# The opening of a three-block transformer kernel reordered, with the third block's position bias computed in it

## Chip, cores and metric

The kernel runs on one core of a Trainium2 chip. The metric is the device time of one execution in microseconds. Before the change it is 779.05 us, the median of 3 runs (778.85 to 779.05).

## The reference

256 tokens of width 1024 (`x`) and 256 context tokens (`ctx`) go through two attention blocks with adaptive norms, and the result through a third block:

```
shift, scale, gate = adaln(c, ada_w[i], ada_b[i])         # silu(c) @ w + b, three parts
h  = rms_norm(x, pre_g[i]) * (1.0 + scale) + shift        # hc likewise from ctx and c_ctx
q, k, v, z = split(h @ a_w_in[0])                         # block 1: differential attention, rope
x = x + gate * rms_norm(y, post_g[i])
...
bias = rel_bias[t5_bucket(idx - qpos)]                    # block 3: bias of the sparse attention
```

The change touches block 1's opening (modulation, first norm, first projection `h @ a_w_in`), the order of its loads, and the matmul that turns `rel_bias` (32 x 8) into one row of 512 position biases for each head. What is computed is the same.

## The kernel before, in words

All matmuls of projections are three products of rounded parts (fp32r): an operand is rounded (`act_hi`, `w_hi`) and its rest kept (`act_lo`, `w_lo`); hi by hi, hi by lo and lo by hi are summed in PSUM. ScalarE writes the `w_hi`, VectorE the `w_lo`.

Work goes by chunks of 512 weight columns. A chunk's weights come in two halves of 512 rows (1 MiB each). Stage `in0` is block 1's input projection: eight chunks, each for four token tiles (0 and 1 are x, 2 and 3 the context) and eight row blocks k. A unit (c, t) is chunk c for tile t, 24 matmuls. Chunks 1 to 4 (`BY_FEATURES`) hold queries and keys: their units come out by features, and VectorE rotates them (`rotate0`, `rest_x`).

Loads: SP issues them in the order of `loads_plan` into `RAW` = 6 buffers. Load n goes to buffer n % 6 and waits in `stream` (L631) until load n - 6 has been used, by the table `emptied` (L587 to L598): the first half of an `in0` chunk is used when its last tile has done k = 3, the second when the chunk's last unit is done. `ada1` is the modulation of block 2: four chunks of two loads, each multiplied by TensorE in `ada_half` (L879) after the unit that `BESIDE_IN0` names. It needs no rounding. `ada0g` is block 1's gate, summed on VectorE by `gate_block` (L2266).

The halves are rounded in the order in which they are used, at fixed places in the queues of ScalarE and VectorE: in `unit_in0` a chunk's first unit is followed by the split of the first half of the next chunk, and `run_chunk` puts the split of its second half ahead of the chunk's last unit. Both engines work in the order written. So whoever waits for a half there holds all units behind it.

```
emptied, firsts = {}, 0
for n, (stage, c, h) in enumerate(loads):
...
    if n >= RAW:
        sp.wait_ge(*emptied[n - RAW])
...
    if t == 0:
        split_through(half_no[("in0", c, 0)] + 2)
```

In the opening chunk 0 is woven by hand (L1024 to L1054) with block 1's modulation `ada0`: four chunks n, each in two halves (`ada_half`), giving shift and scale for the row blocks 2n and 2n + 1. For each n the norm of x and of the context is transposed (`norm0_part`, L1011), the modulation rows are copied by ScalarE and turned into columns (`mod_columns`, L914), VectorE adds the biases (`first_sums`, L2154), ScalarE applies them (`first_hi`, L1449), VectorE takes the rest (`first_lo`, L2174), and only then can TensorE multiply these two blocks. `round_block` (L1466) and `split_block` (L2190) round chunk 0's weights by row block. `stay_awake` (L997) are filler matmuls with zeroes, whose result nobody reads.

The bias of block 3 is a matmul at L1195, ahead of the chunk `in2` 0. Its one-hot matrix is loaded before `in2`'s first load, `rel_bias` in POOL's list (L1990), ScalarE copies the result (`toep`, L1807) and SP writes it to DRAM, from where it is read back in overlapping rows.

Of the kernel before, what the change touches and what calls it, by code (L numbers as in the profile page):

```python
# [14 lines left out]
KT = D // P  # L15
# [44 lines left out]
BESIDE_IN0 = {(c, 3): ("ada1", c) for c in range(4)}  # L60


COLUMNS_IN0 = (4, 1)
# [96 lines left out]
def banks_plan():  # L160
# [33 lines left out]
    for i, (s, n) in enumerate([(0, 0), (0, 1), (1, 0), (1, 1), (0, 2), (1, 2), (0, 3), (1, 3)]):  # L194
        put(("norm0", s, n), 2 + i % 3)
    for t in range(NT):
        put(("in0", 0, t), [0, 1, 7, 5][t])
    for c in range(6):
        for t in range(NT):
            if c in BY_FEATURES:  # L200
                put(("in0", c, t), 2 + t)
            elif c:
                gemm_unit("in0", c, t)
            if (c, t) == (0, 3):
                put(("ada1", 3, 0), 6)
            elif (c, t) == COLUMNS_IN0:
                put(("mod1",), 7)
# [41 lines left out]
    put(("bias",), 6)  # L249
# [50 lines left out]
def block_kernel(nc, a, out):  # L300
# [7 lines left out]
    with ctx:  # L308
# [81 lines left out]
        onehot = v_flat[0:32, 3072:3584]  # L390
        toep = v_flat[0:HEADS, 3584:4096]
# [59 lines left out]
        N_CIN, N_VEC, N_LATE = 3, 4, 10  # L451
# [173 lines left out]
        def _(sp):  # L625
# [26 lines left out]
            load(ident[:], a["k_ident"], s_cin)  # L652
            modulation(0)
            stream(0)
            for t in range(XT):
                load(xs[:, XT + t, :], a["ctx"][0, t * P:(t + 1) * P, :], s_ctxin)
            modulation(1)
            modulation(2)
            stream(1)
            modulation(3)  # L660
            for n in range(2, RAW):
                stream(n)
            for n in range(RAW, len(loads)):
                if loads[n] == ("ada1", 1, 0):

# [24 lines left out]
                if loads[n] == ("in2", 0, 0):  # L690

                    b, at = place[("pv1", XT * HEADS - 1)]
                    sp.wait_ge(full[b], at + 1)
                    load(onehot, a["k_onehot"], s_onehot)
                if loads[n] == ("in2", 3, 0):

                    b, at = place[("bias",)]
                    sp.wait_ge(free[b], at + 1)
                    sp.dma_start(toep_dram, toep).then_inc(s_toepw, 16)
# [121 lines left out]
        def _(pe):  # L821
# [211 lines left out]
            for t in range(XT):  # L1033
                gemm_unit("in0", 0, t, ks=range(0, 2))
            ada_half("ada0", 1, 0)
            stay_awake(5, 4)
            for n in range(2):
                norm0_part(n, 1)
            for n in range(1, 4):
                before = range(2 * n - 2, 2 * n)  # L1040
                ada_half("ada0", n, 1)
                if n > 1:
                    for s in range(2):
                        norm0_part(n, s)
                gemm_unit("in0", 0, 2, ks=before)
                mod_columns(0, n)
                if n < 3:
                    ada_half("ada0", n + 1, 0)
                gemm_unit("in0", 0, 3, ks=before)
                if n < 3:  # L1050
                    for t in range(XT):
                        gemm_unit("in0", 0, t, ks=range(2 * n, 2 * n + 2))
            for t in range(XT):
                gemm_unit("in0", 0, t, ks=range(6, KT))  # L1054
# [137 lines left out]
            pe.wait_ge(s_late, 16 * N_LATE)  # L1192
            pe.wait_ge(s_onehot, 16)
            o = begin(("bias",))
            pe.matmul(o[0:HEADS, :], relb[:], onehot, start=True, stop=True).then_inc(bank_full(("bias",)), 1)  # L1195
# [216 lines left out]
        def _(act):  # L1412
# [53 lines left out]
            def round_block(h, kk):  # L1466


                g, at = h, load_no[halves[h]]
                act.wait_ge(landed[at % RAW], landed_at[at])  # L1470
# [56 lines left out]
            round_block(0, 2)  # L1527
            round_block(0, 3)
            act.wait_ge(s_ctxin, 16 * XT)
            norm0_square(2)  # L1530
            norm0_square(3)
            first_hi(0, 1)
            move(mod_rows(0, 1), ("ada0", 1, 0), n=P)
            first_hi(1, 0)
            first_hi(1, 1)
# [26 lines left out]
            def unit0(c, t):  # L1562
# [7 lines left out]
                if (c, t) == (HALF_KT, 0):  # L1570
                    move(mod_rows(1, HALF_KT - 1), ("ada1", HALF_KT - 1, 0))
# [235 lines left out]
            move(toep, ("bias",))  # L1807
# [153 lines left out]
        def _(pool):  # L1961
# [19 lines left out]
            for dst, src in ((sel[:], a["k_sel"]), (lamb[:], a["a_lambda"][0].partition_broadcast(P)),  # L1981
# [4 lines left out]
                             (w_ukv[:, 0, :], a["w_uk_2"][0]), (w_ukv[:, 1, :], a["w_uv_2"][0]),  # L1986
                             (relb[:], a["rel_bias_2"])):
# [6 lines left out]
        def _(dve):  # L1994
# [179 lines left out]
            def first_lo(n, s):  # L2174
                name = ("norm0", s, n)
                tokens = tile_cols(XT * s, XT)
                dve.wait_ge(*seq.last)
                for i, k in enumerate((2 * n, 2 * n + 1)):
                    if i:
                        dve.wait_ge(s_hi0, feature0_no(s, k) + 1)  # L2180
                        seq.freed(dve.tensor_scalar(sc[:, 4 + k % 4, tokens], psum[:, place[name][0], tile_cols(XT * i, XT)],
                                                    mod[:, 0, 0, k, s:s + 1], mod[:, 0, 1, k, s:s + 1], ALU.mult, ALU.add)
                                  .then_inc(bank_free(name), 1), name)
                        dve.wait_ge(*seq.last)
                    else:
                        dve.wait_ge(s_f0, 2 * n + s + 1)
                    seq.note(dve.tensor_tensor(act_lo[:, k, tokens], sc[:, 4 + k % 4, tokens], act_hi[:, k, tokens].bitcast(F32),  # L2187
                                               ALU.subtract).then_inc(s_lo0, 1), s_lo0)
# [14 lines left out]

            first_sums(0)
            split_block(0, 0)
            split_block(0, 1)
            first_lo(0, 0)
            split_block(0, 2)
            split_block(0, 3)
            norm_in("norm0", range(XT, NT))  # L2210
            first_lo(0, 1)
            first_sums(1)
            first_lo(1, 0)
            first_lo(1, 1)
# [3 lines left out]
            first_lo(2, 0)  # L2218
            first_lo(2, 1)
# [3 lines left out]
            first_lo(3, 0)  # L2223
            first_lo(3, 1)
# [41 lines left out]
            def gate_block(c, s, k):  # L2266
# [3 lines left out]
                if kk == 0 and not s:  # L2270
# [3 lines left out]
                    elif not h:  # L2274
                        dve.wait_ge(s_gatein, 32)
                w = raw_view(load_no[("ada0g", c, h)])[:, kk, :] if c else gate_place[h][:, kk, :]
# [753 lines left out]
```

## Time and profile before

| | us |
|---|---|
| median of 3 runs | 779.05 |
| the profiled execution's own time | 778.93 |
| its span, first to last instruction | 776.8 |
| TensorE busy | 765.9 (99%) |
| VectorE busy | 550.8 (71%) |
| ScalarE busy | 392.8 (51%) |

The busy times are of one profiled execution. Matmuls are pipelined, so their busy time counts overlaps and is no measure of the array at its peak. SPq is the time in which SP issues a transfer, not the transfer. "DMA share" is the mean busy share of the core's 16 DMA engines.

### The profile page before, as it was taken

What the parts mean: (1) busy time and instruction counts of PE and PEld (TensorE: products, weight loads), DVE (VectorE), ACT (ScalarE), POOL (GpSimd) and SP (SyncE); (2) the same over time, 40 slices, a digit from 0 to 9 for tenths busy, and PEclk for the clock granted to TensorE, in tenths of its full rate; (3) what the DMA queues carried; (4) which work ended last, traced back from release to release, by engine and by line L of the source; (5) the groups of instructions that cost most, each with busy time, mean ns of one, the idle gap of its engine ahead of it and who ended that gap; (6) DMA issues with size and microseconds to landing.
All of it is one profiled execution on the core that took longest, in us unless ns stands there. A gap on an engine that the chain in (4) does not pass through costs nothing.

```text
span 776.8 us, 11220 instructions
## 1 busy us (share of the span) xinstructions
PE 765.9 (99%) x4137; PEld 614.1 (79%) x4137; DVE 550.8 (71%) x985; ACT 392.8 (51%) x749; POOL 42.0 (5%) x55
## 2 busy tenths in 40 slices
PE   8999999999999999999999999999999999999998
PEld 6668777887777788867788888787788888888886
DVE  3455998987677867599757766998977554554553
ACT  4462223338788765556656656634444444434341
POOL 0120000000001010111100002200100000000000
PEclk9999999999999999999999999999999999999999
DMA  9995555333000085149221054963325845665611
GB/s 326 360 381 186 212 217 189 113 122 118 2 1 1 1 327 209 60 162 349 70 94 58 9 183 166 376 203 107 109 66 178 271 163 165 206 209 181 205 63 55
DMA packets 72409, 125.78 MB, mean 162 GB/s; under 512 B 2842, under 2 KB 36844, under 8 KB 71204
## 3 DMA queue, kind: packets, MB, share of 16 engines
q1 hardware_dynamic: 71504, 123.00, 45.8%
q10 hardware_dynamic: 388, 1.08, 0.4%
q0 software_dynamic: 464, 0.98, 0.4%
q8 instruction: 34, 0.56, 0.3%
q14 instruction: 19, 0.16, 0.1%
HBM read 123.99 MB, written 1.06 MB: 161 GB/s over the span
## 4 chain that ended last, share of the span: by engine, by line
PE 83%; DVE 8%; ACT 3%; DMA 3%; issue 2%; SPq 0%; POOL 0%; DVEq 0%; ACTq 0%
PE psum L871 18%; PE psum L873 17%; PE psum L872 16%; PE psum L1067 3%; PE psum L1092 3%; DMA raw<-in_a_w_in 3%; PE psum L993 3%; PE psum L1387 3%; PE psum L1388 3%; PE psum L1386 3%; PE psum L860 2%; PE psum L1165 2%; PE psum L861 2%; PE psum L862 2%; DVE w_lo L2004 2%
## 5 line engine op out<-in xcount | busy, mean ns | idle before, releaser
L872 PE MATMUL psum<-w_lo,act_hi 128*128 128x512 f32 (+1 forms) x624 | 242.0, 388 | 0.0
L871 PE MATMUL psum<-w_hi,act_hi 128*128 128x512 f32 (+1 forms) x584 | 237.5, 407 | 2.6 <-DVE act_lo L2187 2.4
L873 PE MATMUL psum<-w_hi,act_lo 128*128 128x512 f32 (+1 forms) x584 | 227.0, 389 | 0.0
L2004 DVE TENSOR_TENSOR w_lo<-raw,w_hi 128x2048 fp32r<-128x2048 f32 (+1 forms) x68 | 153.2, 2261 | 62.1 <-ACT w_hi L1425 62.1
L1425 ACT ACTIVATE w_hi<-raw 128x2048 fp32r<-128x2048 f32 (+1 forms) x72 | 136.3, 1896 | 65.5 <-PE psum L873 30.9
L871 PEld LDWEIGHTS psum<-w_hi,act_hi 128*128 128x128 f32 x584 | 109.7, 188 | 37.2 <-issue 13.3
L872 PEld LDWEIGHTS psum<-w_lo,act_hi 128*128 128x128 f32 x624 | 117.5, 188 | 20.5 <-issue 0.5
L873 PEld LDWEIGHTS psum<-w_hi,act_lo 128*128 128x128 f32 x584 | 109.6, 188 | 23.4
L1973 POOL TENSOR_TENSOR rstd<-ms,half_neg 128x1 f32<-128x1 f32 (+3 forms) x38 | 35.5, 936 | 520.6 <-DVE ms L2045 520.5
L860 PE MATMUL psum<-act_hi,w_hi 128*128 128x512 f32 x128 | 50.6, 395 | 0.5 <-DVE w_lo L2004 0.5
L861 PE MATMUL psum<-act_lo,w_hi 128*128 128x512 f32 x128 | 50.0, 390 | 0.0
L862 PE MATMUL psum<-act_hi,w_lo 128*128 128x512 f32 x128 | 49.8, 389 | 0.0
L1583 ACT ACTIVATE sc<-psum,nmax 128x512 f32<-128x512 f32 (+1 forms) x64 | 36.8, 587 | 20.3 <-DVE nmax L2320 20.3
L1498 ACT ACTIVATE sc<-psum 128x512 f32<-128x512 f32 (+1 forms) x59 | 30.8, 523 | 16.3 <-PE psum L993 9.2
L2320 DVE TENSOR_REDUCE nmax<-psum 128x2 f32<-128x1024 f32 (+1 forms) x32 | 30.5, 955 | 10.3 <-PE psum L1067 10.2
L1387 PE MATMUL psum<-w_lo,act_hi 128*128 128x512 f32 x88 | 34.2, 389 | 0.0
L1929 ACT ACTIVATE sc<-psum 128x256 f32<-128x256 f32 x22 | 8.4, 384 | 50.5 <-PE psum L873 50.5
L860 PEld LDWEIGHTS psum<-act_hi,w_hi 128*128 128x128 f32 x128 | 24.0, 188 | 9.2 <-issue 3.4
L1386 PE MATMUL psum<-w_hi,act_hi 128*128 128x512 f32 x80 | 31.2, 390 | 0.0
L1388 PE MATMUL psum<-w_hi,act_lo 128*128 128x512 f32 x80 | 31.1, 389 | 0.0
L993 PE MATMUL psum<-ident,sc 128*128 128x128 f32 x184 | 29.5, 274 | 0.4 <-ACT sc L1884 0.4
L1092 PEld LDWEIGHTS psum<-vbuf,sc 128*128 128x128 f32 x192 | 26.1, 191 | 4.0 <-ACT sc L1498 0.9
(295 smaller groups left out, 1124.7 us busy)
## 6 DMA issues: line engine op xcount, KB each, us to landing
raw<-in_a_w_in SPq DMA_DIRECT2D x16, 1024.0 KB, 9.3
raw<-in_ada_w SPq DMA_DIRECT2D x14, 1024.0 KB, 5.2
raw<-in_w_out SPq DMA_DIRECT2D x12, 1024.0 KB, 5.5
raw<-in_w_gate SPq DMA_DIRECT2D x22, 512.0 KB, 4.1
raw<-in_w_up SPq DMA_DIRECT2D x22, 512.0 KB, 5.2
raw<-in_w_down SPq DMA_DIRECT2D x11, 1024.0 KB, 4.9
raw<-in_b_w_in SPq DMA_DIRECT2D x10, 1024.0 KB, 7.6
raw<-in_w_in SPq DMA_DIRECT2D x10, 1024.0 KB, 6.1
```

The lines of the kernel that those rows point to most:

```text
L860: pe.matmul(o, hi[:, tile_cols(t)], act_hi[:, k, :], start=(k == 0), stop=False)
L861: pe.matmul(o, hi[:, tile_cols(t)], act_lo[:, k, :], start=False, stop=False)
L862: mm = pe.matmul(o, lo[:, tile_cols(t)], act_hi[:, k, :], start=False, stop=(k == KT - 1))
L871: pe.matmul(oh, x_hi, hi, start=(k == 0), stop=False)
L872: pe.matmul(o[:, 0:n], x_hi, lo, start=False, stop=False)
L873: mm = pe.matmul(oh, x_lo, hi, start=False, stop=(k == KT - 1))
L993: mm = pe.transpose(o[:, tile_cols(i)], src[:, tile_cols(i)], ident[:])
L1386: pe.matmul(oh, x_hi, hi, start=(j == 0 and i == 0), stop=False)
L1387: pe.matmul(o, x_hi, lo, start=False, stop=False)
L1388: mm = pe.matmul(oh, x_lo, hi, start=False, stop=(last and i == 1))
L1425: ins = act.activation(hi, weights, ACTF.Copy)
L2004: ins = dve.tensor_tensor(rest, weights, hi.bitcast(F32), ALU.subtract)
```

## The change

- `BESIDE_IN0` puts the four `ada1` chunks behind in0's chunks 1 to 4 instead of 0 to 3. `loads_plan` follows it, so the order of loads moves too. The column turn of `ada1` goes from behind unit (4, 1) to behind (5, 1).
- The first weight half comes in two transfers of 0.5 MiB, rows k = 0 and 1 before the context, k = 2 and 3 behind the second `ada0` chunk; the first has a semaphore of its own.
- SP's opening: chunk 1 of in0 now stands before `ada1`, the gate's first chunk before `ada1` 0.
- TensorE's opening: units by row block, then tile (`first_units`); x's units of a row block before, the context's behind the modulation; four fillers less. ScalarE and VectorE are put in the same order.
- The bias: one-hot and `rel_bias` are loaded by SP behind the context, into `gate0`; the matmul stands in the opening in PSUM bank 5, with copy and write behind it. `gate_block` waits for the write.

```
-BESIDE_IN0 = {(c, 3): ("ada1", c) for c in range(4)}
+BESIDE_IN0 = {(c + 1, 3): ("ada1", c) for c in range(4)}
-COLUMNS_IN0 = (4, 1)
+COLUMNS_IN0 = (5, 1)
...
-        onehot = v_flat[0:32, 3072:3584]
-        toep = v_flat[0:HEADS, 3584:4096]
+        onehot = gate0[0:32, 1, 0:COLS]
+        toep = gate0[0:HEADS, 1, COLS:]
...
             modulation(0)
-            stream(0)
+            sp.dma_start(raw_view(0)[:, 0:2, :], first[:, 0:2, :]).then_inc(s_firstin, 16)
             for t in range(XT):
                 load(xs[:, XT + t, :], a["ctx"][0, t * P:(t + 1) * P, :], s_ctxin)
+            load(relb[:], a["rel_bias_2"], s_onehot)
+            load(onehot, a["k_onehot"], s_onehot)
             modulation(1)
+            sp.dma_start(raw_view(0)[:, 2:4, :], first[:, 2:4, :]).then_inc(landed[0], 16)
             modulation(2)
             stream(1)
             modulation(3)
-            for n in range(2, RAW):
-                stream(n)
-            for n in range(RAW, len(loads)):
-                if loads[n] == ("ada1", 1, 0):
+            b, at = place[("bias",)]
+            sp.wait_ge(free[b], at + 1)
+            sp.dma_start(toep_dram, toep).then_inc(s_toepw, 16)
+            for n in range(2, len(loads)):
+                if loads[n] == ("ada1", 0, 0):
...
+            X, CONTEXT = range(XT), range(XT, NT)
+            first_units(X, (0, 1))
             ada_half("ada0", 1, 0)
-            stay_awake(5, 4)
...
+            pe.wait_ge(s_onehot, 32)
+            o = begin(("bias",))
+            pe.matmul(o[0:HEADS, :], relb[:], onehot, start=True, stop=True).then_inc(bank_full(("bias",)), 1)
+            norm0_part(0, 1)
+            ada_half("ada0", 1, 1)
+            norm0_part(1, 1)
+            mod_columns(0, 1)
+            first_units(CONTEXT, (0, 1))
+            first_units(X, (2,))
+            ada_half("ada0", 2, 0)
+            first_units(X, (3,))
+            ada_half("ada0", 2, 1)
...
+            mod_columns(0, 3)
+            first_units(CONTEXT, (4, 5))
+            first_units(X, (6, 7))
```

Three places show how instructions moved. The first is SP's queue from chunk 4 of in0 to the first half of chunk 6 (rows on `raw` with 128x4x512 from `in_a_w_in` are in0's halves; `in_ada_w` with 128x2048 is `ada1`, with 128x4x512 `ada0g`). Before:

```order
L638 DMA raw<-in_ada_w 128x2048 [waits w_first_half_used]
L638 DMA raw<-in_ada_w 128x2048 [waits bank5_full]
L638 DMA raw<-in_a_w_in 128x4x512 [waits ada_first_half_used] x2
L638 DMA raw<-in_ada_w 128x4x512 [waits w_first_half_used]
L638 DMA raw<-in_ada_w 128x4x512 [waits bank5_full]
L638 DMA raw<-in_a_w_in 128x4x512 [waits ada_first_half_used]
L638 DMA raw<-in_a_w_in 128x4x512 [waits bank6_full]
L638 DMA raw<-in_a_w_in 128x4x512 [waits w_first_half_used]
```

And in the change:

```order
L639 DMA raw<-in_a_w_in 128x4x512 [waits ada_first_half_used] x2
L639 DMA raw<-in_ada_w 128x2048 [waits w_first_half_used]
L639 DMA raw<-in_ada_w 128x2048 [waits bank5_full]
L639 DMA raw<-in_ada_w 128x4x512 [waits ada_first_half_used] x2
L639 DMA raw<-in_a_w_in 128x4x512 [waits w_first_half_used]
L639 DMA raw<-in_a_w_in 128x4x512 [waits bank5_full]
L639 DMA raw<-in_a_w_in 128x4x512 [waits ada_first_half_used]
```

Before, chunk 5's two halves (sixth and seventh row) wait for an `ada1` pair, and chunk 6's first half (last row) for the first-half use of chunk 4. Now chunk 5's first half is the one that waits for the first-half use (fifth row), and chunk 5's second half for the end of chunk 4's last unit in bank 5.

The second place is TensorE behind the first four units of chunk 0 (`kT` holds the modulation's second chunk). Before:

```order
L908 MATMUL psum<-kT,cstat 32x128 [waits bank6_free,ada0_landed2]
L908 MATMUL psum<-kT,cstat 32x128 x15
L1001 MATMUL psum<-w_hi 128x512 x4
L1019 MATMUL psum<-ident,zbuf 128x128 [waits xn_ready]
L1019 MATMUL psum<-ident,zbuf 128x128 x3
L1019 MATMUL psum<-ident,zbuf 128x128 [waits bank2_free,xn_ready]
L1019 MATMUL psum<-ident,zbuf 128x128 x3
L908 MATMUL psum<-kT,cstat 32x128 [waits ada0_landed3]
```

And in the change:

```order
L904 MATMUL psum<-kT,cstat 32x128 [waits bank6_free,ada0_landed2]
L904 MATMUL psum<-kT,cstat 32x128 x15
L1039 MATMUL psum<-gate,relb 8x512 [waits onehot_in]
L1015 MATMUL psum<-ident,zbuf 128x128 [waits xn_ready]
L1015 MATMUL psum<-ident,zbuf 128x128 x3
L904 MATMUL psum<-kT,cstat 32x128 [waits ada0_landed3]
L904 MATMUL psum<-kT,cstat 32x128 x15
L1015 MATMUL psum<-ident,zbuf 128x128 [waits bank2_free,xn_ready]
L1015 MATMUL psum<-ident,zbuf 128x128 x3
L917 MATMUL psum<-ident,gate 128x128 [waits bank6_free]
```

The bias matmul stands where the fillers stood, and the column turn (last row) directly behind the modulation's second half.

The third is ScalarE from unit (4, 0) of in0 on, in the change (`round_k` from PSUM is a unit's context part, from `sc` the x part of the unit before):

```order
L1567 ACTIVATE round_k<-psum 128x256 [waits bank2_full]
L1428 ACTIVATE w_hi<-raw 128x2048 [waits bank5_full,raw_landed2]
L1560 ACTIVATE round_k<-sc 128x256 [waits x_features_rotated]
L1567 ACTIVATE round_k<-psum 128x256 [waits bank3_full]
L1560 ACTIVATE round_k<-sc 128x256 [waits x_features_rotated]
L1567 ACTIVATE round_k<-psum 128x256 [waits bank4_full]
L1428 ACTIVATE w_hi<-raw 128x2048 [waits w_first_half_used,raw_landed3]
```

The rounding of chunk 5's first half (second row) stands behind unit (4, 0) and ahead of (4, 1), as before the change; only the copy of `ada1`'s rows, which stood between the two, is gone from here.

## Rows read from the trace of the kernel before

**Rows 1.** Engine totals of the page: busy us, share of the span, instructions.

```profile
PE 765.9 (99%) x4137; PEld 614.1 (79%) x4137; DVE 550.8 (71%) x985; ACT 392.8 (51%) x749; POOL 42.0 (5%) x55
```

**Rows 2.** Stretches: us, busy of PE, PEld, DVE, ACT, POOL, PEclk, DMA share, GB/s.

```profile
1.47:56.75 55.28, 51.56 (x447) 37.34 (x447) 25.17 (x63) 28.63 (x52) 7.42 (x12) 1.00 1.05 363
56.75:108.00 51.25, 50.82 (x240) 38.89 (x236) 41.78 (x72) 12.56 (x19) 1.59 (x3) 1.00 0.56 211
```

**Rows 3.** TensorE's waits, then its timeline (start, us), both from 0 to 57 us.

```profile
PE psum L871 <- DVE act_lo L2187: 2.4, 3, 1.4
...
PE psum L908 <- DVE mod L2164: 0.8, 2, 0.4
...
1.47 6.42 PE L1001 MATMUL psum<-w_hi 128*128 128x512 f32 x16 [1.47 <-DVE w_hi L2113]
...
11.02 2.33 PE L1001 MATMUL psum<-w_hi 128*128 128x512 f32 x9
...
18.33 0.47 PE L871 MATMUL psum<-w_hi,act_hi 128*128 128x512 f32 x1 [1.35 <-DVE act_lo L2187]
...
22.55 1.20 PE L1001 MATMUL psum<-w_hi 128*128 128x512 f32 x4
...
54.90 1.92 PE L908 MATMUL psum<-raw,cstat 128*32 128x512 f32 x16
56.75 0.50 PE L860 MATMUL psum<-act_hi,w_hi 128*128 128x512 f32 x1
```

**Rows 4.** The chain that ended last (start, us, what), from 0 to 110 us.

```profile
4.29 11.27 DMA raw<-in_a_w_in
...
56.02 10.61 DMA raw<-in_a_w_in
...
68.61 2.30 DVE w_lo L2004
```

**Rows 5.** SP's timeline at 128 and 149 us, and landing times of each first issue.

```profile
128.49 1.23 SPq L638 DMA_DIRECT2D raw<-in_a_w_in  x2
...
raw<-in_a_w_in SPq DMA_DIRECT2D x1, 1024.0 KB, 7.0
...
149.12 0.37 SPq L638 DMA_DIRECT2D raw<-in_a_w_in  x1
...
raw<-in_a_w_in SPq DMA_DIRECT2D x1, 1024.0 KB, 5.3
```

**Rows 6.** ScalarE's timeline at 135 us, VectorE's from 138 to 175 us.

```profile
135.79 1.92 ACT L1425 ACTIVATE w_hi<-raw 128x2048 fp32r<-128x2048 f32 x1
...
138.84 2.29 DVE L2004 TENSOR_TENSOR w_lo<-raw,w_hi 128x2048 fp32r<-128x2048 f32 x1
...
144.63 0.25 DVE L2144 TENSOR_TENSOR mod<-psum,cols 128x16 f32<-128x16 f32 x2
...
145.20 1.01 DVE L2282 TENSOR_SCALAR gate<-raw,cols 128x512 f32<-128x512 f32 x2
...
151.29 2.29 DVE L2004 TENSOR_TENSOR w_lo<-raw,w_hi 128x2048 fp32r<-128x2048 f32 x1
...
174.14 0.75 DVE L2335 SCALAR_TENSOR_TENSOR sc<-sc,rinv 128x512 f32<-128x512 f32 x1
```

**Rows 7.** TensorE's timeline from 148 to 175 us.

```profile
148.93 0.39 PE L860 MATMUL psum<-act_hi,w_hi 128*128 128x512 f32 x1
...
154.37 0.39 PE L871 MATMUL psum<-w_hi,act_hi 128*128 128x512 f32 x1
...
174.95 0.66 PE L993 MATMUL psum<-ident,sc 128*128 128x128 f32 x4
```

**Rows 8.** TensorE's timeline from 466 to 476 us, and one row of VectorE's.

```profile
466.99 1.02 PE L1195 MATMUL psum<-vbuf,relb 32*8 32x512 f32 x2
...
475.74 1.09 PE L966 MATMUL psum<-ident,zbuf 128*128 128x128 f32 x8
...
474.40 1.28 DVE L2470 SCALAR_TENSOR_TENSOR zbuf<-xs,rstd,gate 128x1024 f32<-128x1024 f32 x1 [0.44 <-POOL rstd L1973]
```

More of the change, by code:

```diff
@@ L195, in banks_plan @@
         put(("norm0", s, n), 2 + i % 3)
+    put(("bias",), 5)
     for t in range(NT):
@@ L248, in banks_plan @@
         gemm_unit("out1", c, t)
-    put(("bias",), 6)
     for t in range(XT):
@@ L652, in _ @@
             load(ident[:], a["k_ident"], s_cin)
+            first = half_src(*loads[0])[0]
             modulation(0)
-            stream(0)
+            sp.dma_start(raw_view(0)[:, 0:2, :], first[:, 0:2, :]).then_inc(s_firstin, 16)
             for t in range(XT):
                 load(xs[:, XT + t, :], a["ctx"][0, t * P:(t + 1) * P, :], s_ctxin)
+            load(relb[:], a["rel_bias_2"], s_onehot)
+            load(onehot, a["k_onehot"], s_onehot)
             modulation(1)
+            sp.dma_start(raw_view(0)[:, 2:4, :], first[:, 2:4, :]).then_inc(landed[0], 16)
             modulation(2)
@@ L689, in _ @@
                     load(gain3, a["norm2_w_2"][0].partition_broadcast(P), s_gain3)
[L690 to L699, printed above, removed]
                 if loads[n] == ("in2", 5, 0):
@@ L1189, in _ @@
             gemm_unit("out1", 1, 1, SECOND)
[L1192 to L1195, printed above, removed]
             gemm_unit("in2", 0, 0)
@@ L1469, in round_block @@
                 g, at = h, load_no[halves[h]]
-                act.wait_ge(landed[at % RAW], landed_at[at])
+                if h == 0 and kk < 2:
+                    act.wait_ge(s_firstin, 16)
+                else:
+                    act.wait_ge(landed[at % RAW], landed_at[at])
                 hi, weights = (part[:, kk * COLS:(kk + 1) * COLS] for part in split_parts(g)[0][0:2])
@@ L1531, in _ @@
             norm0_square(3)
+            move(toep, ("bias",))
             first_hi(0, 1)
             move(mod_rows(0, 1), ("ada0", 1, 0), n=P)
+            round_block(0, 2)
             first_hi(1, 0)
+            round_block(0, 3)
             first_hi(1, 1)
@@ L1806, in _ @@
             split()
-            move(toep, ("bias",))
             norm_square("norm2", 1, NT + 1)
@@ L2172, in first_sums, with first_lo @@
                                                   op0=ALU.add, op1=ALU.mult).then_inc(s_mod, 1), s_mod)
-            def first_lo(n, s):
-                name = ("norm0", s, n)
+            def first_lo(n, s, block):
+                name, k = ("norm0", s, n), 2 * n + block
                 tokens = tile_cols(XT * s, XT)
-                dve.wait_ge(*seq.last)
[L2178 to L2188, printed above, removed]
+                if block:
+                    dve.wait_ge(s_hi0, feature0_no(s, k) + 1)
+                    seq.freed(dve.tensor_scalar(sc[:, 4 + k % 4, tokens], psum[:, place[name][0], tile_cols(XT, XT)],
+                                                mod[:, 0, 0, k, s:s + 1], mod[:, 0, 1, k, s:s + 1], ALU.mult, ALU.add)
+                              .then_inc(bank_free(name), 1), name)
+                else:
+                    dve.wait_ge(s_f0, 2 * n + s + 1)
+                dve.wait_ge(*seq.last)
+                seq.note(dve.tensor_tensor(act_lo[:, k, tokens], sc[:, 4 + k % 4, tokens], act_hi[:, k, tokens].bitcast(F32),
+                                           ALU.subtract).then_inc(s_lo0, 1), s_lo0)
             def split_block(h, kk):
@@ L2202, in split_block, with first_los @@
                     done_halves[0] += 1
+            def first_los(n):
+                for part in range(2):
+                    for block in range(2):
+                        first_lo(n, part, block)
             first_sums(0)
             split_block(0, 0)
+            first_lo(0, 0, 0)
             split_block(0, 1)
-            first_lo(0, 0)
+            first_lo(0, 0, 1)
+            norm_in("norm0", range(XT, NT))
+            for block in range(2):
+                first_lo(0, 1, block)
+            first_sums(1)
             split_block(0, 2)
+            first_lo(1, 0, 0)
+            first_lo(1, 0, 1)
             split_block(0, 3)
[L2210 to L2214, printed above, removed]
+            for block in range(2):
+                first_lo(1, 1, block)
             first_sums(2)
```

52 lines of the change are left out of this document (21 added, 31 removed).

## The prediction, made blind

> **What bounds the kernel now.** I read the engine totals first: TensorE is busy 99% of the span [rows 1]. Time is won or lost only where TensorE waits, runs filler, or could start earlier. Then the table by stretches [rows 2]: until 56.75 us the DMA engines are full (share 1.05 at 363 GB/s) while TensorE is busy 51.56 of 55.28 us; from 56.75 to 108 us the share falls to 0.56 and VectorE is busy 41.78 of 51.25 us. So the opening is tied to the order of the bytes, and the chunks behind it to VectorE.
>
> TensorE's waits and its order of time [rows 3] show what the opening wastes: 2.4 us for `act_lo` (1.35 of it before the first product at 18.33), 0.8 us for `mod`, and four fillers, 1.20 us, at 22.55. The `ada1` rows begin at 54.90, chunk 1 at 56.75. The chain of waits [rows 4] goes from there through a transfer that lands at 66.63 (56.02 + 10.61), its rounding, and its rest on VectorE at 68.61.
>
> **The opening, part by part.** The sum is worked in the time of the profiled execution (778.93 us), 0.12 below the median 779.05.
> - The first quarter of chunk 0's weights now comes ahead of the next. That is 0.5 MB less before the first block: its landing at 15.56 (4.29 + 11.27) [rows 4] moves up 1.4 us at 363 GB/s. Then the modulation is last, not the weights: I put the first product at 17.6 instead of 18.33. In the order by block, the first four units end 1.0 us earlier.
> - The four fillers (1.0 us net of overlap) go; the bias pair, 1.02 us [rows 8], takes their place: about 0.
> - The context's products now lie over the modulation of each pair of blocks. What goes: the rest of the wait for `act_lo`, 1.05 us; the 0.8 us for `mod` with 0.5 us of drained pipe around it; 0.5 us of short gaps between units. 2.85 us. The first column turn now comes right behind its copy: minus 0.2.
> - Sum: 1.0 + 2.85 - 0.2 = 3.65 us. The `ada1` rows (54.90 to 56.75, 1.85 us) go behind chunk 1, so chunk 1 starts 5.5 us earlier, at 51.2.
>
> Does VectorE follow? The first half of chunk 2 has 2 MiB (2.1 MB) fewer ahead of it, since one `ada1` pair now comes behind it: 5.8 us at 363 GB/s, landing at 60.9 instead of 66.63. VectorE's chain from 68.61 on moves up by 5.8 and is the later of the two, so 5.8 counts. The column turn of `ada1` (0.5 us) goes from chunk 4 to chunk 5. So the point at which k = 3 of chunk 4's last tile is done (the next matmul starts at 148.93 [rows 7]) moves up by 5.8 + 0.5 = 6.3 us.
>
> **What the shift of `ada1` does to the ring.** Load n waits until load n - 6 has been used. Before, chunk 5's halves (loads 20 and 21) follow `ada1` pair 3 (14 and 15), done before chunk 4 begins; they are issued at 128.49 and the first lands after 7.0 us [rows 5], at 135.49. ScalarE rounds it at 135.79 [rows 6]: 0.3 us in hand. In the change pair 3 goes behind chunk 4, loads 14 and 15 are chunk 4 itself, and load 20 waits for k = 3 of chunk 4's last tile, as the order of SP's rows shows. Before, that event released chunk 6's first half: issued at 149.12, landed after 5.3 us [rows 5]. I give chunk 5's first half this place.
>
> Behind it, in the clock of before:
> - Landing 149.12 + 5.3 = 154.4; `w_hi` 1.92 [rows 6] and hand-over, 156.4; `w_lo` 2.29, 158.7. TensorE wants it 2.72 us after 148.93 and 1.85 of `ada1` rows later, at 153.5. First stall 5.2 us, then 2.7 us of products.
> - ScalarE and VectorE both stand at that split, which is written in their queues behind unit (4, 0). Units (4, 1) and (4, 2) with two gate blocks are queued behind it, and the split of the second half behind them. From the end of the first `w_lo` (138.84 + 2.29) to that of the second (151.29 + 2.29) took 12.45 us [rows 6]; without the `mod` sums (0.57, to 145.20), which move away, 11.9. So the second ends at 170.6. TensorE wants it at 158.8 + 2.7 = 161.5: second stall 9.1 us. Before, that product started at 154.37 [rows 7] with no wait.
> - On to the first turn of the attention. VectorE: from 153.58 to the first probabilities at 174.89 (174.14 + 0.75) [rows 6] 21.3 us, and 0.6 of moved `mod` sums: 192.5. TensorE: from 154.37 to 174.95 [rows 7] 20.6 us, and the moved column turn 0.5: 191.8 before any loss of clock.
>
> **Clock.** No row shows TensorE behind stalls of 5 and 9 us. Near the start sixteen fillers took 6.42 us, 0.40 each; nine later ones 2.33 us [rows 3], which for sixteen would be 4.1 or less by their step. The table gives 1.00 for the whole stretch [rows 2]. So the price lies between 0 and about 2.6 us; I take the middle, 1.3, since these stalls resemble the idle start more than the short waits behind it: TensorE at 193.1, and VectorE's 192.5 is covered.
>
> The Trainium skill, page "TensorE: Matmul & The Clock Gate", section on the HAM clock gate, states that idle time puts the array's clock at half rate and that activity lifts it again. The slow fillers agree, the clock column does not, and no run here shows such a stall. By the rule the price is above 0; with none at all VectorE's 192.5 would set the point, 0.6 us less.
>
> **The sum:** 193.1 - 174.95 - 6.3 = 11.85 us later. From there every load is released by a step of the engines, and nothing gives it back.
>
> **The bias taken from the third block.** The pair at 466.99 goes, 1.02 us. The next norm turn is at 475.74, straight behind VectorE's `zbuf` (474.40 + 1.28) [rows 8], so the time becomes idle there: I take 0.1 us, between 0 and 1.0. ScalarE's copy of the row has no reader waiting. The write from `gate0` (16 KB) is issued once SP is through its opening loads, and the gate sums that wait for it come behind the `w_lo` at 68.61 less 5.8 [rows 4]; its cover is some 25 us. The 64 KB of one-hot rows cost 0.2 us of queue, within the 1.4 us that the split gives.
>
> Total: 778.93 + 11.85 - 0.1 = 790.7, as a median 790.8.
>
> **Rivals.**
> 1. The gain stays (faster). If chunk 5 were not late, 3.65 us would be kept: 775.3. One event decides: the load must be issued 16.2 us (170.6 - 154.37) ahead of 149.12, by 132.9. For it speak the full DMA engines and the waits of the opening [rows 2, 3]; against it the release in SP's order and the 0.3 us in hand. Chance 0.06.
> 2. Only the first stall counts, since VectorE catches up: 5.2 - 3.65 = 1.5 later, 780.6. VectorE's rows stand close in that stretch [rows 6], so 0.04.
> 3. The opening gives nothing, since the bytes up to chunk 0's last operand are the same and the DMA engines are full (1.05): 3.65 more, 794.4. But TensorE's waits there are for `act_lo` and `mod`, not for transfers [rows 3]. Chance 0.1.
>
> **Numbers.** The forecast has 0.8; its own range is 788.3 to 793.3 (clock 1.3 either way, landing 0.4, opening 1, bias 0.9). The range of 787.0 to 795.5 takes in rival 3 and leaves out 0.1 for rivals 1 and 2 and about as much for prices that I mis-sized. 0.2% (1.6 us) is about what a measurement can tell from no change: faster 0.06, same 0.04 (rival 2, at that edge), slower 0.90.
>
> **What would show it.** Chunk 1 starting near 51; chunk 2's first half landing near 61; SP issuing chunk 5 near 143 instead of 128.49; ScalarE idle for some 18 us in chunk 4 on a transfer of `raw`; TensorE idle 5 us before chunk 5 and 9 us inside its first unit; the first attention turn near 187. If chunk 5 is issued near 123, the forecast is wrong.

## The result and the profile after

The changed kernel takes 793.18 us, the median of 4 runs (792.53 to 793.27), against 779.05 for the kernel before (4 runs, 778.85 to 779.80): ratio 1.0179, 95% interval 1.0167 to 1.0192. It is slower by 14.1 us. Its profiled execution took 793.27 us, with a span of 791.2.

The engine totals of the page, as in [rows 1]:

```profile
PE 768.2 (97%) x4133; PEld 616.7 (78%) x4133; DVE 550.7 (70%) x985; ACT 392.5 (50%) x749; POOL 41.7 (5%) x54
```

No engine has more instructions, and TensorE's busy time rises by 2.3 us only. So most of the 14 us is waiting. TensorE's waits from 0 to 200 us (total, times, longest), against [rows 3]:

```profile
PE psum L867 <- DVE w_lo L2009: 12.0, 2, 6.5
PE psum L856 <- DVE w_lo L2009: 1.7, 2, 0.9
...
PE psum L904 <- DMA kT<-in_ada_w: 1.1, 1, 1.1
...
PE psum L867 <- DVE act_lo L2190: 0.3, 1, 0.3
```

The waits for `act_lo` (2.4) and `mod` (0.8) of [rows 3] have nearly gone. Two new ones, 12.0 us together, have come. TensorE's timeline shows where both stand, with the opening first:

```profile
17.11 0.47 PE L867 MATMUL psum<-w_hi,act_hi 128*128 128x512 f32 x1 [0.30 <-DVE act_lo L2190]
...
23.87 1.08 PE L904 MATMUL psum<-kT,cstat 128*32 128x128 f32 x32 [1.06 <-DMA kT<-in_ada_w]
...
51.50 0.39 PE L856 MATMUL psum<-act_hi,w_hi 128*128 128x512 f32 x1
...
55.20 0.50 PE L856 MATMUL psum<-act_hi,w_hi 128*128 128x512 f32 x1 [0.81 <-DVE w_lo L2009]
...
104.17 0.50 PE L856 MATMUL psum<-act_hi,w_hi 128*128 128x512 f32 x1 [0.86 <-DVE w_lo L2009]
...
147.31 1.92 PE L904 MATMUL psum<-raw,cstat 128*32 128x512 f32 x16
154.69 0.77 PE L867 MATMUL psum<-w_hi,act_hi 128*128 128x512 f32 x1 [5.45 <-DVE w_lo L2009]
...
159.52 0.63 PE L869 MATMUL psum<-w_hi,act_lo 128*128 128x512 f32 x1
166.66 0.80 PE L867 MATMUL psum<-w_hi,act_hi 128*128 128x512 f32 x1 [6.51 <-DVE w_lo L2009]
...
176.72 0.60 PE L917 MATMUL psum<-ident,sc 128*128 128x128 f32 x4
...
189.59 0.60 PE L989 MATMUL psum<-ident,sc 128*128 128x128 f32 x4
```

The first product comes at 17.11 instead of 18.33, chunk 1 at 51.50 instead of 56.75. Of these 5.25 us, 1.85 are the `ada1` rows that moved away, so the opening gained 3.4. The first turn of the attention (the transposes of the first probabilities, last row above) is at 189.59 instead of 174.95 [rows 7]: 14.64 later. In the whole execution 14.34 are left (793.27 - 778.93), so the whole loss is there by this point.

The chain of waits from 144 us on says what holds both products:

```profile
144.70 5.59 DMA raw<-in_a_w_in
150.31 1.92 ACT w_hi L1428
152.25 2.30 DVE w_lo L2009
...
155.10 0.42 DVE sc L2257
...
158.23 0.50 DVE gate L2293
...
164.40 2.21 DVE w_lo L2009
166.66 0.80 PE psum L867
```

A transfer that was not issued before 144.70 (128.49 in [rows 5]), its rounding, its rest; then a whole unit's rotations and gate sums, which stand in VectorE's queue between the two halves; then the second rest. ScalarE's row for it is

```profile
150.31 1.91 ACT L1428 ACTIVATE w_hi<-raw 128x2048 fp32r<-128x2048 f32 x1 [18.82 <-DMA raw<-in_a_w_in]
```

18.82 us of idle time on a transfer, where [rows 6] shows none. The table by stretches (us, busy of PE, PEld, DVE, ACT, POOL, PEclk, DMA share, GB/s) shows that bandwidth is not what is short:

```profile
150.00:155.00 5.00, 0.31 (x1) 0.34 (x2) 2.64 (x2) 2.49 (x3) 0.00 (x0) 0.83 1.04 395
155.00:160.00 5.00, 5.00 (x12) 3.46 (x11) 4.63 (x11) 2.50 (x3) 0.00 (x0) 0.50 0.51 189
160.00:165.00 5.00, 0.15 (x1) 0.00 (x0) 4.67 (x11) 0.69 (x2) 0.00 (x0) 0.84 0.00 0
165.00:170.00 5.00, 3.34 (x8) 2.67 (x9) 4.71 (x9) 0.00 (x0) 0.00 (x0) 0.50 0.00 0
```

From 160 to 170 us the DMA engines do nothing. The column before them, PEclk, is the granted clock: 0.50, the lower of its two levels, 1.2 GHz, while TensorE works between and behind the stalls.

### The profile page after: what moved, and what is told of

Same layout as the page of the kernel before. It is cut to its first block, busy times and chain, and to the rows that moved or that the text cites. A ratio compares the mean times of both kernels' runs of the same rounds, so it can differ in the third digit from the quotient of the medians.

```text
span 791.2 us, 11213 instructions
## 1 busy us (share of the span) xinstructions
PE 768.2 (97%) x4133; PEld 616.7 (78%) x4133; DVE 550.7 (70%) x985; ACT 392.5 (50%) x749; POOL 41.7 (5%) x54
## 3 DMA queue, kind: packets, MB, share of 16 engines
q10 hardware_dynamic: 388, 1.08, 0.4%
HBM read 123.99 MB, written 1.06 MB: 158 GB/s over the span
## 4 chain that ended last, share of the span: by engine, by line
PE 69%; DVE 16%; SPq 5%; ACT 3%; DMA 3%; issue 2%; POOL 0%; DVEq 0%; ACTq 0%
PE psum L867 14%; PE psum L869 13%; PE psum L868 13%; DVE w_lo L2009 4%; DMA raw<-in_a_w_in 3%; PE psum L1074 3%; PE psum L1099 3%; PE psum L1391 3%; PE psum L1390 3%; PE psum L1389 3%; SPq L649 3%; PE psum L989 2%; PE psum L1172 2%; DVE sc L2257 2%; PE psum L856 2%
## 5 line engine op out<-in xcount | busy, mean ns | idle before, releaser
L867 PEld LDWEIGHTS psum<-w_hi,act_hi 128*128 128x128 f32 x584 | 110.7, 190 | 46.6 <-issue 16.9
```

The costliest lines, as they stand in the source:

```text
L867: pe.matmul(oh, x_hi, hi, start=(k == 0), stop=False)
```

## The experiments

Twelve kernels were tried, built from the change or from the kernel before. "Before" in each comparison is the kernel before on the same chip, 778.5 to 779.1 us.

**1. The shift of `ada1` undone, the opening kept.**

```
-BESIDE_IN0 = {(c + 1, 3): ("ada1", c) for c in range(4)}
-COLUMNS_IN0 = (5, 1)
+BESIDE_IN0 = {(c, 3): ("ada1", c) for c in range(4)}
+COLUMNS_IN0 = (4, 1)
```

> The change with the shift of ada1 undone (ada1 0 to 3 again beside chunks 0 to 3, its column turn behind (4, 1), the loads in the order that follows from it); the new opening and the bias in it stay. My theory: the loss comes from the shift alone, through the release of chunk 5's first half. Then the second stall goes (chunk 5's first half issued before 132, no wait of TensorE over 1 us at 150 to 170), but the first half of chunk 2 stands behind an ada1 pair again and lands near 66.6, so VectorE's chain behind it is where it was before the change. TensorE, ahead by some 3.5 us, gives them back in a wait for w_lo inside chunk 3 (near 104 to 108): about 779, the same as the kernel before within 0.2%. Rival A: the opening's gain does not depend on that chain: 775.4, the wait inside chunk 3 under 0.5 us. Rival B: the opening or the bias cause the loss: near 793, with chunk 5 in time.

Measured: 779.81 us, ratio 1.001 (1.0001 to 1.0019), 0.7 us over the kernel before. The stalls are gone and so is the gain, as expected, but not where I expected. TensorE and ScalarE:

```profile
58.91 0.50 PE L856 MATMUL psum<-act_hi,w_hi 128*128 128x512 f32 x1 [2.29 <-DVE w_lo L2009]
```

```profile
54.55 1.92 ACT L1428 ACTIVATE w_hi<-raw 128x2048 fp32r<-128x2048 f32 x1 [2.38 <-DMA raw<-in_a_w_in]
...
67.83 1.92 ACT L1428 ACTIVATE w_hi<-raw 128x2048 fp32r<-128x2048 f32 x1 [3.89 <-DMA raw<-in_a_w_in]
```

Already chunk 1's second half, for which nobody waited before, lands too late with `ada1` 0 ahead of it; chunk 2's follows at 67.83, 1.2 us later than before. So the opening's gain needs the new order of bytes: the two parts of the change are not independent.

**2. The shift alone, in the kernel before.**

```
-BESIDE_IN0 = {(c, 3): ("ada1", c) for c in range(4)}
+BESIDE_IN0 = {(c + 1, 3): ("ada1", c) for c in range(4)}
```

> The kernel before with the shift of ada1 and nothing else. My theory: the two stalls of the change appear whole, with nothing from the opening to set against them, except that VectorE's chain starts earlier: TensorE reaches (4, 3) at the earliest where it did before less the ada1 pair, and chunk 5's first half is issued when k = 3 of (4, 3) is done. Waits of 5 to 6 us before chunk 5 and 6 to 7 us in its first unit; time near 795, at least 793. Rival: the loss comes from the opening or the bias; then this kernel is at 779, with no wait over 1 us at chunk 5.

Measured: 796.57 us, ratio 1.0222 (1.0208 to 1.0236). Waits and time of issue:

```profile
PE psum L869 <- DVE w_lo L2002: 12.7, 2, 7.1
```

```profile
146.73 4.97 SPq L638 DMA_DIRECT2D raw<-in_a_w_in  x4
```

The shift carries the whole loss: alone it costs 17.5 us (796.57 against 779.07), 1.6 more than I expected. The other parts of the change are worth 796.57 - 793.18 = 3.4 us on top of it, the 3.4 that the start of chunk 1 shows.

**3. The second chunk of the gate not loaded.** This tests the ring by itself: `ada1`'s products stay where the change put them, and load numbers behind the gate shrink by two.

```
-        if c == 4:
-            plan += both("ada0g", 1)
...
-                w = raw_view(load_no[("ada0g", c, h)])[:, kk, :] if c else gate_place[h][:, kk, :]
+                w = act_hi[:, 4 * h + kk, :].bitcast(F32) if c else gate_place[h][:, kk, :]
```

> The change with the second of the two chunks of block 1's gate (ada0g 1) not loaded; its sum on VectorE reads other data of the same size instead, so half of block 1's gate is left out. No work of an engine goes, only two loads of 1 MiB, and with them the numbering of the ring behind them: chunk 5's first half takes a number two lower and waits for the half two loads earlier, ada1 pair 2, instead of for k = 3 of (4, 3). My theory (the ring's release, not the place of ada1's products, makes the stalls): both stalls go, the opening's gain stays in part, and the time is near 777.0, between 775.3 and 779. Rival A: the stalls come from where ada1's products and its column turn stand or from VectorE's load in chunk 4: no change, 792 to 793. Rival B: the bytes matter, not the release: 2 MiB less of transfer moves chunk 5's landing by 5.8 us at most, so some 5.8 us off the second stall, near 787.

Measured: 776.40 us, ratio 0.9966 (0.9954 to 0.9978). Both stalls are gone, and SP issues chunk 5 with the loads behind it from 125.43 on:

```profile
125.43 25.11 SPq L637 DMA_DIRECT2D raw<-in_a_w_in  x6
```

Rival A falls: the products stand where they stood. Rival B falls too: it allowed 5.8 us, and 16.8 went. What remains is the release.

**4. The gate's second chunk loaded two places later.** Experiment 3 with nothing left out:

```
-        if c == 4:
+        if c == 5:
             plan += both("ada0g", 1)
...
-SUMMED_IN0.update({(4, 1): [(1, 0), (1, 1)], (5, 0): [(1, 2), (1, 3), (1, 4)], (5, 1): [(1, 5), (1, 6), (1, 7)]})
+SUMMED_IN0.update({(5, 0): [(1, 0), (1, 1), (1, 2), (1, 3)], (5, 1): [(1, 4), (1, 5), (1, 6), (1, 7)]})
```

> The change with one thing moved: the two loads of the gate's second chunk stand behind chunk 5's in the order of loads instead of ahead of them, and its sums on VectorE go to units (5, 0) and (5, 1), four row blocks each. Chunk 5's first half then waits for ada1 pair 2, used near 121, and not for chunk 4. No byte is left out. My theory: both stalls go, as they went where the gate's second chunk was not loaded; VectorE has two more sums (2.55 us) between (5, 0) and the first probabilities, where it was the later engine, so part of the gain is given back: near 777.5, between 776 and 779. Rival A: the gate's halves, now released by chunk 4, land only near 160 and VectorE stands at them with the rounding of chunk 6 behind: 781 or more, with an idle time of VectorE on a transfer near 158. Rival B: the place of ada1's rows costs as well: over 785.

Measured: 776.44 us, ratio 0.9967 (0.9956 to 0.9979), faster than the kernel before. SP, VectorE and TensorE:

```profile
124.24 1.24 SPq L639 DMA_DIRECT2D raw<-in_a_w_in  x2
```

```profile
162.44 6.26 DVE L2291 SCALAR_TENSOR_TENSOR gate<-raw,cols,gate 128x512 f32<-128x512 f32 x8
```

```profile
173.12 0.66 PE L989 MATMUL psum<-ident,sc 128*128 128x128 f32 x4 [0.20 <-DVE sc L2346]
```

Chunk 5 is issued 20.5 us earlier than in the change (144.70), and the 14 us become a gain of 2.6. The later sums make VectorE the last at the first turn, but by 0.20 us only; I had allowed more.

**5. `ada1` 0 and 1 out of the ring.** They are loaded into the buffer of x, which is free between the first norm and the residual; the products stand behind (1, 3), (2, 2), (2, 3) and (3, 3).

```
-BESIDE_IN0 = {(c + 1, 3): ("ada1", c) for c in range(4)}
+BESIDE_IN0 = {(1, 3): ("ada1", 0), (2, 2): ("ada1", 1), (2, 3): ("ada1", 2), (3, 3): ("ada1", 3)}
...
+                if loads[n] == ("ada1", 2, 0):
+                    sp.wait_ge(s_xn, NT)
+                    for h in range(2):
+                        load(beside_place[h], half_src("ada1", 0, h)[0], s_beside[0])
```

> The change, but the loads of ada1 0 and 1 go to the buffer of x, which is free behind the first norm, instead of through the ring, ada1 0 behind chunk 2's first loads; ada1 stands behind (1, 3), (2, 2), (2, 3) and (3, 3), its column turn behind (4, 1) again. So every half of in0 from chunk 2 on is issued as early as the ring allows, and none of them waits for chunk 4. My theory: the opening's gain and the earlier chain of VectorE both count, with no stall at chunk 5: first half of chunk 2 landing near 57 instead of 62.7, no wait of TensorE over 1 us between 57 and 175, and 775.1, faster than both kernels. Rival A: VectorE's chain is bound by its own work, not by the landing: TensorE waits 2 to 4 us inside chunk 3 or 4 and the time is 777 to 779. Rival B: the DMA engines, full until chunk 4, deliver chunk 4 or 5 late by the 2 MiB that now come ahead: waits for transfers of raw, 779 or more.

Measured: 776.01 us, ratio 0.9968 (0.9957 to 0.9978). ScalarE at chunk 2, TensorE's first turn:

```profile
58.76 1.91 ACT L1442 ACTIVATE w_hi<-raw 128x2048 fp32r<-128x2048 f32 x1
```

```profile
172.15 0.66 PE L1003 MATMUL psum<-ident,sc 128*128 128x128 f32 x4
```

No stall. The landing no longer limits chunk 2: ScalarE rounds it at 58.76 without idle time on a transfer. But 3.0 us are gained, not the 3.9 that I expected. The start of chunk 1, at 51.73 here, gains 3.2 besides the 1.85 of the moved rows, and 0.81 of it is lost at once: the wait at 55.42 for the rest of chunk 1's second half, which the change has too (at 55.20 above).

**6. That wait taken away**, on top of experiment 5: ScalarE rounds chunk 1's second half behind chunk 0's first copy.

```
-                    if t == tiles[-1] and not before_norm:
+                    if t == (1 if (stage, c) == ("in0", 0) else tiles[-1]) and not before_norm:
                         split_through(g0 + 3)
```

> The kernel with ada1 0 and 1 in the buffer of x, and in addition ScalarE rounds chunk 1's second half two copies earlier, behind chunk 0's first copy instead of its third. Measured there: a wait of 0.81 us for this half's w_lo at 55.42, behind an idle time of VectorE of 1.90 us. My theory: this wait is why the opening's gain of 3.4 us at the start of chunk 1 was 2.6 behind it and the kernel came to 776.0 instead of 775.1; without it 775.2. Rival A: the transfer lands just before 50, so rounding earlier in order changes nothing: 776.0. Rival B: the two copies that wait behind the rounding hold their banks, and chunk 1's third unit waits for one: 776.5 to 777.

Measured: 774.68 us, ratio 0.9945 (0.9933 to 0.9958), the fastest kernel here. VectorE takes both rests in a row (the idle time of 1.90 us between them is gone), and the first turn is 1.2 us earlier than in experiment 5:

```profile
48.83 4.65 DVE L2023 TENSOR_TENSOR w_lo<-raw,w_hi 128x2048 fp32r<-128x2048 f32 x2 [0.72 <-ACT w_hi L1442]
```

```profile
170.99 0.66 PE L1003 MATMUL psum<-ident,sc 128*128 128x128 f32 x4
```

That is more than the 0.81 of the wait. It fits with chunk 2's rounding, which begins 1.15 us earlier (57.61 against 58.76).

**7. The same line on top of experiment 4.**

> The change with the gate's second chunk loaded behind chunk 5 (measured alone: 776.44) and ScalarE rounding chunk 1's second half behind chunk 0's first copy (worth 1.33 us on the kernel with ada1 in the buffer of x: 776.01 to 774.68). My theory: the wait of 0.81 us at 55.2 goes here too, but VectorE's chain from chunk 2 on is set by the landing of its first half near 62, which does not move, and TensorE gives the gain back in a wait for w_lo near 104, which grows from 0.6 to 1.4 us; so most of it is lost: 776.2, between 775.8 and 776.5. Rival: the gain of 1.3 us holds: 775.1.

Measured: 776.18 us, ratio 0.997 (0.9959 to 0.9981): the gain is lost as expected, but the wait that was to show it is not there. TensorE waits only 0.3 us in all for `w_lo` from chunk 1 on. This execution's modulation arrived later (a wait of 1.37 us at 21.70), and chunk 1 starts at 52.37, 0.87 later than in experiment 4, which uses up what the removed wait gave. The first turn waits for VectorE, as in experiment 4. The rounding of chunk 2's first half, in experiment 4 and then here, and the first turn here:

```profile
62.40 1.92 ACT L1428 ACTIVATE w_hi<-raw 128x2048 fp32r<-128x2048 f32 x1 [3.77 <-DMA raw<-in_a_w_in]
```

```profile
61.88 1.92 ACT L1428 ACTIVATE w_hi<-raw 128x2048 fp32r<-128x2048 f32 x1 [3.48 <-DMA raw<-in_a_w_in]
```

```profile
172.56 0.66 PE L989 MATMUL psum<-ident,sc 128*128 128x128 f32 x4 [0.19 <-DVE sc L2346]
```

From that rounding to the first turn both take 110.7 us (173.12 - 62.40 and 172.56 - 61.88), and both times it waits for the transfer. So in these two executions the landing of chunk 2 sets the first turn, and an earlier `w_lo` of chunk 1 can't move it.

**8. Fillers in the two stalls of the change**, to price the clock: 22 matmuls before chunk 5's first half, 37 before its second.

> The change with filler matmuls of 128x512, whose result nobody reads, where TensorE stands idle: 22 before chunk 5's first half, 37 before its second, as many as fit into the waits of 5.45 and 6.51 us. My theory: in the change the granted clock falls to 0.50 in and behind both stalls, and the matmuls that run at half rate cost some 1.9 us; with fillers the clock stays at 1.00 in every window from 150 to 175, the two waits stay (as fillers), and the first attention turn comes at 188.3, where VectorE's first probabilities set it, instead of 189.6: minus 1.3, near 791.9. Rival: the slow matmuls lie beside VectorE's work and cost nothing on the path: 793.2, the first turn at 189.6 as before. Second rival: the fillers stand in front of products that were ready, plus 0.5 to 1 us: 794.

Measured: 791.26 us, ratio 1.0158 (1.0144 to 1.0172). The granted clock is 1.00 in every stretch from 145 to 175 us.

```profile
148.43 5.32 PE L1083 MATMUL psum<-act_hi,ones 128*128 128x512 f32 x22
...
156.40 8.55 PE L1083 MATMUL psum<-act_hi,ones 128*128 128x512 f32 x37
165.54 0.50 PE L867 MATMUL psum<-w_hi,act_hi 128*128 128x512 f32 x1 [0.59 <-DVE w_lo L2014]
...
173.84 0.60 PE L917 MATMUL psum<-ident,sc 128*128 128x128 f32 x4
...
187.23 0.66 PE L989 MATMUL psum<-ident,sc 128*128 128x128 f32 x4 [0.37 <-DVE sc L2351]
```

Part of the 1.9 us between 793.18 and 791.26 is not the clock: in this execution chunk 2 landed 0.8 us earlier (its rounding begins at 61.96 instead of 62.74) and chunk 5's transfer took 0.4 us less, so the second `w_lo` starts at 163.20 instead of 164.32:

```profile
163.20 2.29 DVE L2014 TENSOR_TENSOR w_lo<-raw,w_hi 128x2048 fp32r<-128x2048 f32 x1
```

```profile
164.32 2.29 DVE L2009 TENSOR_TENSOR w_lo<-raw,w_hi 128x2048 fp32r<-128x2048 f32 x1
```

So I compare within the chain. From the first `w_lo` to the second it is 12.06 us here (163.20 - 151.14) and 12.07 in the change (164.32 - 152.25): the slow matmuls between the stalls cost nothing. From the second half's first product to the column turn TensorE needs 8.30 us here (173.84 - 165.54) and 10.06 in the change (176.72 - 166.66): the slow clock costs it 1.76. From the start of the second `w_lo` to the first turn it is 24.03 against 25.27: 1.24 reach the path, and then VectorE is last, by 0.37.

**9. The bias computed in the third block again**, on top of experiment 5.

> The kernel with ada1 0 and 1 in the buffer of x, and the bias of the third block computed in the third block again (its loads, matmul, copy and write as in the kernel before). My theory: the bias's place is worth nothing either way: in the opening its 1.02 us lie in TensorE's wait for the second half of a modulation chunk (1.06 to 1.4 us, longer without it), in the third block in front of a wait for VectorE. So 776.0 plus or minus 0.3. Rival A: the move saved its 1.02 us in the third block: 777.0. Rival B: it costs in the opening (matmul, and 80 KB of loads before the modulation's second chunk): 775.2.

Measured: 776.27 us (775.51 to 777.08), ratio 0.9964 (0.9952 to 0.9977), against 776.01 for experiment 5. No difference can be told: where the bias stands is worth less than these executions, 1.6 us apart, can show.

**10. The first weight half in one transfer again**, on top of experiment 5.

> The kernel with ada1 0 and 1 in the buffer of x, with the first weight half loaded whole again at the place of its first two row blocks. My theory: the modulation's first half is behind the same bytes as before, but the second modulation chunk and the context stand behind 0.5 MiB more (1.4 us), so the first product or the next modulation rows start some 1.0 us later and the third copy of chunk 0, with which VectorE's chain begins, as well: 777.0, between 776.5 and 777.5. Rival: the bytes up to the last operand of chunk 0 are the same and the waits only change places: 776.0, within 0.2.

Measured: 777.15 us, ratio 0.9982 (0.9973 to 0.9991). The first product is at 17.63 with 1.20 us of wait, instead of 16.94 with 0.30:

```profile
17.63 0.47 PE L875 MATMUL psum<-w_hi,act_hi 128*128 128x512 f32 x1 [1.20 <-DVE act_lo L2198]
```

Chunk 1 starts at 52.96 instead of 51.73. The split into quarters is worth some 1.1 us, a third of the opening's gain.

**11 and 12. Fillers ahead of the second modulation chunk**, on the kernels of experiments 5 and 6. Both are about single executions that took longer; the last section tells of them.

```
             first_units(X, (0, 1))
+            stay_awake(5, 2)
             ada_half("ada0", 1, 0)
...
             norm0_part(0, 1)
+            begin(("in0", 0, XT))
+            stay_awake(7, 3)
             ada_half("ada0", 1, 1)
```

> The kernel with ada1 0 and 1 in the buffer of x, with five fillers ahead of the second modulation chunk, two before its first half and three before its second. Single executions of that kernel fell into two groups: 775.6 to 776.7 at a mean clock of 1.000 and 777.8 to 777.9 at 0.998 (2 of 7); in two other kernels' profiles this half was followed by matmuls at a granted clock of about 0.5 behind a wait of 1.5 and 1.6 us. My theory: these executions are those in which the transfer comes late enough for the clock to fall; with fillers in the wait, no execution has a clock under 0.999 or a time over 777.2, and the median stays at 776.0 or rises by up to 0.4 where the transfer was early. Rival: the late transfer itself makes the slower group, not the clock: times up to 777.9 again, at a clock of 1.000.

> The fastest kernel so far (ada1 0 and 1 in the buffer of x, chunk 1's second half rounded behind chunk 0's first copy, 774.68) with the same five fillers. My theory: it had no execution of the slower group in 5, so there is little to save: 774.7 to 775.1, clock 0.999 or more in every execution. Rival: the fillers stand in front of transfers that are there: 775.5.

Measured: 776.12 (775.88 to 776.31), ratio 0.9967 (0.9954 to 0.9979), with a mean clock of 1.000 in all five executions; and 775.21 (774.68 to 776.91), ratio 0.9953 (0.9939 to 0.9966), where the execution of 776.91 had 0.998. Its trace was taken, and the slow stretch is at another wait, ahead of the first modulation chunk:

```profile
10.66 1.08 PE L918 MATMUL psum<-act_hi_as_f,cstat 128*32 128x128 f32 x32 [1.86 <-DMA act_hi_as_f<-in_ada_w]
11.67 3.91 PE L1011 MATMUL psum<-w_hi 128*128 128x512 f32 x9
```

Nine fillers took 3.91 us, where [rows 3] has 2.33. The five executions of the first kernel lie closer together than without fillers; the second kernel's median is 0.5 us above that of experiment 6, over the 775.1 that I had allowed.

## Why the prediction was right, point by point

I said 790.8 us, between 787.0 and 795.5, slower with a chance of 0.90. It came to 793.2. The mechanism and its two places were right; the forecast was 2.4 us short, mostly by two terms of the sum, 1.9 us in the landing of chunk 2 and 0.5 in the clock. Both err the same way, so the forecast did not come near by errors that cancel.

- **The opening, 3.65 us.** 3.4 at the start of chunk 1. The first product came at 17.11, 0.5 before my 17.6. I overlooked that TensorE, now earlier, would wait for the second modulation chunk (1.06 us at 23.87), and that chunk 1's own second half would be late for a TensorE that comes early: 0.81 us at 55.20. In the change it cost nothing further, since VectorE's chain was the later one behind it; in the kernel of experiment 5 it was worth 1.3 (experiment 6).
- **"So 5.8 counts": the term that failed most.** Chunk 2's first half was rounded at 62.74 (66.66 before): 3.9 earlier, not 5.8. The stretches up to each landing:

```profile
0.00:66.60 66.60, 61.41 (x490) 45.49 (x491) 30.31 (x71) 29.02 (x53) 9.36 (x21) 1.00 1.02 360
```

```profile
0.00:62.70 62.70, 58.74 (x474) 44.96 (x475) 30.19 (x71) 29.55 (x54) 9.12 (x20) 1.00 1.02 352
```

  That is 23.98 MB before and 22.07 MB now: 1.9 MB less, 5.3 us at 360 GB/s. But the rate was 352, and 22.07 MB at 352 instead of 360 take 1.4 us more. I had taken one rate for both. How much of this is the change's and how much this one execution's stays open: with the same opening this rounding began at 61.77 in experiment 3, 62.40 in experiment 4, 61.88 in experiment 7 and 61.96 in experiment 8, so 4.3 to 4.9 us earlier than before. None comes near 5.8. From there all moved as the forecast said: the product at 104.17 (108.06 before) waits for VectorE, and chunk 5 is issued at 144.70 instead of 149.12, 4.4 earlier and not 6.3. This explains 1.9 of the 2.8 us by which the first turn (189.59) missed my 186.8; the rest is 0.3 of a longer transfer, 0.5 of clock and about 0.1 along VectorE's chain. Behind the turn 0.3 of it came back.
- **The ring.** Chunk 5's first half is released by k = 3 of chunk 4's last tile. Experiments 3 and 4 show it: the same bytes and products with another release, and both stalls are gone. The landing took 5.59 instead of 5.3.
- **The stalls.** For the first I said 5.2, and 5.45 was measured. For the second I said 9.1. The first products of the two halves are 11.97 us apart; less 2.72 for 12 matmul steps at full clock that is 9.25. At the slow clock the twelve took 5.46 us to the end of the last (154.69 to 159.52 + 0.63), so the page shows 6.51 of wait and not 9.25.
- **The clock, 1.3 us between 0 and 2.6.** TensorE lost 1.76 behind the second stall, and 1.24 of it reached the path (experiment 8). The term was 0.5 too small, and what I said of VectorE holds: without the loss it is the next, 0.37 us of waiting in the trace. The stalls did behave like the idle start: 0.43 us from matmul to matmul behind them, 0.40 a filler there [rows 3]. This is also what the Trainium skill says, page "TensorE: Matmul & The Clock Gate", section on the HAM clock gate: idle time puts the array at half rate. This case's trace agrees, with a granted clock of 0.50.
- **The bias, 0.1.** Experiment 9 measures 0.26 with executions that spread over 1.6, so the term can be neither confirmed nor refuted.
- **The rivals.** The gain did not stay and VectorE did not catch up between the halves. The third, that the opening gives nothing, would have given 794.4, closer to the result than my forecast; but for another reason, since the opening gave 3.4 (experiment 2 against the change). Experiment 2, where the opening is the old one, is as good as the kernel of this rival, and it took 796.57. My 794.4 was too low for it also because I added 3.65, which is no term of the sum: without the opening's gain chunk 5's issue moves up by the 1.85 of `ada1` rows and 0.5, 2.35 instead of 6.3, which is 3.95 more. In experiment 2 it moved by 2.4 (146.73).

## What to carry to other kernels

When loads share a ring of buffers in order of use, moving one load moves the release of all that come a ring's length behind it: write down, for each load, which use frees its buffer, before and after, and compare that time with when the load is wanted. Where engines keep their order, a late transfer can cost twice, as here: the work queued behind the late one also held the next. Putting a load that nobody is waiting for behind one that somebody will wait for was enough here to turn a loss of 14.1 us into a gain of 2.6, and taking two loads out of the ring with one rounding moved up gave 4.3.

## What the runs showed of the hardware

Short waits lowered the clock too. In experiment 1 TensorE waited 2.29 us at 58.91, and the matmuls from 60.05 to 62.61 took 0.63 us each instead of 0.39. Behind a wait of 1.63 us in experiment 3 and of 1.49 us in experiment 9, both for the second modulation chunk, 32 small matmuls took 1.94 and 1.81 us instead of 1.08:

```profile
24.47 1.94 PE L902 MATMUL psum<-kT,cstat 128*32 128x128 f32 x32 [1.63 <-DMA kT<-in_ada_w]
```

```profile
23.66 1.81 PE L923 MATMUL psum<-kT,cstat 128*32 128x128 f32 x32 [1.49 <-DMA kT<-in_ada_w]
```

Waits of 1.41 us there (experiment 5) and of 1.53 (experiment 10) had no such effect, so the length of a wait alone doesn't decide. The times fit: of experiment 5's seven executions five took 775.6 to 776.7 us at a mean clock of 1.000 and two 777.8 and 777.9 at 0.998; of experiment 10's eleven, three at 0.998 or less took 778.2 to 778.8, the others 776.7 to 777.6. In experiment 1 they don't: six executions at 0.998 or less took 779.3 to 779.9 us, five at 1.000 took 779.3 to 780.4. The slower executions of experiments 5 and 10 have no trace, so it is argued, not shown, that in them a transfer arrives a little later and costs its delay and the slow matmuls behind it, together 1.5 to 2 us. That the fillers of experiment 11 removed this rests on five executions, and whether they shift the odds on experiment 6's kernel can't be told from five.
